# Value rows of 40 instead of 32 tokens gathered and summed on VectorE in a mixture-of-experts decoder layer

## The chip, the cores and the metric

One Trainium2 chip, one of its cores. The metric is the device time of one execution in microseconds (us), from launch to end; runs of the same kernel vary by some 0.3%. TensorE (PE in the profile) multiplies, VectorE (DVE), ScalarE (ACT) and GpSimd (POOL) do elementwise work, and SyncE (SP) only issues transfers here. GpSimd issues the indirect transfers (gathers and scatters by an index).

## The reference

One decoder layer over 256 tokens of width 1024, in fp32: a mixer (a gated linear recurrence beside attention), a cross-attention into 256 memory tokens, and a PEER channel mixer; then a last RMSNorm. The change lies in the PEER part alone:

```python
q = (t @ w_q).reshape(T, 8, 2, 128)                     # 8 heads, two halves
s = einsum('thpd,hpnd->thpn', q, sub_keys)              # 128 keys a half
s_top, i_top = top_k(s, 16)                             # then the 256 sums of pairs
best_s, pos = top_k(cand_s, 16)                         # 16 experts a head: 128 a token
ids   = ...                                             # i * 128 + j, of 16384 experts
gates = softmax(best_s)
act = gelu(einsum('td,ted->te', x_c, u[ids_c]))
y   = einsum('te,ted->td', gates * act, v[ids_c])
```

Each token uses 128 of 16384 experts. An expert has a row of `u` and a row of `v`, 1024 numbers each.

## The kernel before, in words

**Dense instead of sparse.** The kernel computes all 16384 activations of every token. It goes over j = 0..127; "key" j stands for the 128 experts i * 128 + j, one to a partition. In the *u stage* TensorE computes for each key the scores of 128 experts against 256 tokens (8 chunks of the width, 3 products each, lines 1431 to 1433), ScalarE takes the GELU of them. In the *v stage* it multiplies, for each key, the 128 rows of `v` with the weighted activations and sums over all keys in eight PSUM banks. Weights are exact to fp32 by splitting each operand in a high and a low fp32r part: ScalarE writes the high part (line 702), VectorE the low part (lines 1021 and 1028), so each key needs a load (SP), a split on ScalarE and one on VectorE before TensorE can use it. Four slots rotate: a row is loaded again into a slot as soon as its split is done (SP waits for `s_vl`), and ScalarE splits into a slot when TensorE has finished the key four before (`s_vm`).

**Three kinds of tokens.** What multiplies the activations is a token's gate where it uses the expert, and zero elsewhere.
- `WT` = 192 tokens get it from a map in DRAM, `wmap`, into which GpSimd scatters the gates (line 431, 192 indirect transfers), and which comes back two keys at a time (`wblk`, 64 loads); VectorE multiplies (L1155, function `weigh`; GpSimd does the first four, L437).
- `OT` = 32 tokens (one-hot tokens) get it inside the u stage: from key 95 (`ROUTE0`) on, every second key, a group of `GRP` = 4 tokens. VectorE and ScalarE build two one-hot matrices a token, TensorE multiplies them (L1454, 4 products a group), VectorE places the result (`place`); activations that come after it are multiplied by `late_gelu`.
- `NS` = 32 tokens (sparse tokens) don't take part in the dense product of the v stage. Their activations are stored to DRAM (`adump`, five pieces). When all is there, GpSimd gathers with 32 indirect transfers the activations that each sparse token needs (L447: 128 numbers a transfer, one to a partition), and then with 32 more the rows of `v` (L452: 128 rows of 4 KB, three buffers `vg`). VectorE multiplies each gathered tile by a weight for each partition and adds it up in `acc_s` (L1166, `sparse_fma`). A token has P / NS = 4 partitions, and each of these holds 32 of its 128 experts. Near the end TensorE sums the 4 partitions of each token by a product with a 0/1 matrix `sel` (L1507).

**Columns.** So the v stage has `DT` = 256 - 32 = 224 tokens. For each key and chunk there are two products: high part of `v` with both parts of the activations, 448 columns (L1479), and low part with the high part, 224 columns (L1480). The last two keys are done chunk by chunk, three products of 224 columns each (L1490), so that the end of the kernel can start early.

**Order around the change.** All queues are written by hand. VectorE's loop over keys holds the splits, the remaining routing (top-k) and the gates; the last batch of gates (tokens 128 to 255) comes at key 78. At that point it also copies the sparse tokens' expert numbers and gates to their four partitions (`sparse_rows`: eight copies of 32 partitions). In the v stage VectorE does for each key the low part of `v`, for each second key `weigh` and the low part of the weighted activations (L1150), and the sparse products are laid in by

```python
FMA0, NVG = 34, 3
def fma_step(c):
    return FMA0 + c * (KEYS - 4 - FMA0) // NSD      # 32 steps, keys 34 to 121
```

GpSimd's order in the v stage: four multiplications, 32 activation gathers, then the 32 row gathers, each of which waits until the product three before is done (`s_fma`). SP's order at the end of u: the first four `v` rows, a wait for the scatters, four weight blocks, the last dump.

Of the kernel before, what the change touches and what calls it, by code (L numbers as in the profile page):

```python
# [13 lines left out]
F32 = mybir.dt.float32  # L14
# [8 lines left out]
P = 128  # L23
# [56 lines left out]
def build(nc, x, mem, par, wa, wx, w, keys_t, u_t, v, wmap, adump, xres, out):  # L80
    ctx = ExitStack()
    with ctx:
        base = 16512

        def at(name, off, shape, dt=F32):
            return nc.alloc_sbuf_tensor_at(name, [P] + shape, dt, offset=base + off)

        def sem(name):
            return ctx.enter_context(nc.semaphore(name))
# [4 lines left out]
        act_w = at("act_w", 16 * K, [KEYS, DT])  # L94
# [30 lines left out]
        gate_s = at("gate_s", m + 384, [NSD])  # L125
        idx_v = at("idx_v", m + 512, [NSD], U32)
        idx_a = at("idx_a", m + 640, [NSD], U32)
        late = at("late", m + 768, [2, OT])
        aw_s = at("aw_s", m + 1024, [NSD])
        w_s = at("w_s", m + 1152, [NSD])  # L130
        sel = at("sel", m + 4352, [NS])
        wblk = at("wblk", m + 1280, [2, WBK, WT])
# [37 lines left out]
        def flat(ap):  # L170
# [41 lines left out]
        s_ad, s_ag, s_ws, s_fma, s_al = (sem(n) for n in (  # L212
            "s_act_dumped", "s_act_gathered", "s_sparse_weights", "s_sparse_fma", "s_al_sums"))
# [76 lines left out]
        def vbank(c):  # L290

            return acc[:, c] if c < 4 else bank[c - 4]
# [9 lines left out]
        def _(sp):  # L302
# [77 lines left out]
        def _(pool):  # L380
# [65 lines left out]
            for c in range(NSD):  # L446
                nc.gpsimd.indirect_dma_start(out=aw_s[:, c:c + 1], out_offset=None, in_=adump,  # L447
                                             in_offset=bass.IndirectOffsetOnAxis(ap=idx_a[:, c:c + 1], axis=0)).then_inc(s_ag, 16)
            for c in range(NSD):
                if c >= NVG:  # L450
                    pool.wait_ge(s_fma, c - NVG + 1)
                nc.gpsimd.indirect_dma_start(out=vg[:, c % NVG], out_offset=None, in_=v,  # L452
                                             in_offset=bass.IndirectOffsetOnAxis(ap=idx_v[:, c:c + 1], axis=0)).then_inc(s_vg[c % NVG], 16)
# [334 lines left out]
        def _(dve):  # L788
# [70 lines left out]

            dve.wait_ge(s_spc, 1)  # L860
# [201 lines left out]
            def sparse_rows(dst, src):  # L1062
                nr = NSD // PH
                to, fr = (a.rearrange("p (h k) -> p h k", h=PH) for a in (dst[:], src[:]))
                for r in range(TOPK // nr):
                    last = V.tensor_copy(to[NS * r:NS * r + NS], fr[P - NS:P, :, nr * r:nr * r + nr])
                link(last)

            def gates(b):
# [4 lines left out]
                if t == 1:  # L1074
                    sparse_rows(idx_v, dest)
# [50 lines left out]
            for r in range(P // NS):  # L1126
                q = slice(NS * r, NS * r + NS)
                last = V.tensor_scalar(tcol[q, 2:3], tcol[q, 0:1], float(-NS * r), None, ALU.add)
            link(last)
            V.tensor_scalar(sel[:], iota[:, 0:NS], tcol[:, 2:3], None, ALU.is_equal)  # L1130
# [26 lines left out]
            def sparse_fma(c):  # L1157
                if c == 0:
                    dve.wait_ge(s_ag, 16 * NSD)
                    V.tensor_tensor(w_s[:], gate_s[:], aw_s[:], ALU.mult).then_inc(s_ws, 1)  # L1160
                    dve.wait_ge(s_ws, 1)
                dve.wait_ge(s_vg[c % NVG], 16 * (c // NVG + 1))
                w = w_s[:, c:c + 1]
                if c:
                    dve.wait_ge(s_fma, c)
                    V.scalar_tensor_tensor(acc_s[:], vg[:, c % NVG], w, acc_s[:], ALU.mult, ALU.add).then_inc(s_fma, 1)  # L1166
                else:
                    V.tensor_scalar(acc_s[:], vg[:, 0], w, None, ALU.mult).then_inc(s_fma, 1)

            parts, batches = PARTS0, EARLY  # L1170
            for j in range(KEYS):
# [16 lines left out]
                if j == ROUTE0 - 2:  # L1188
                    dve.wait_ge(s_kte, 1)
                if j + 2 in range(ROUTE0, ROUTE0 + 2 * NGRP, 2):  # L1190
                    onehots_i((j + 2 - ROUTE0) // 2)
# [28 lines left out]
        def _(pe):  # L1220
# [283 lines left out]
            def sparse_sums():  # L1504
                pe.wait_ge(s_fma, NSD)
                for c in range(DC):
                    pe.matmul(vbank(c)[:, DT:T], acc_s[:, P * c:P * c + P], sel[:], start=False, stop=False,  # L1507
                                     skip_group_check=True)
# [65 lines left out]
```

## Time and profile before

| | |
|---|---|
| median of 3 runs | 1010.39 us (1008.94 to 1011.98) |
| the profiled execution | 1010.26 us, span 1008.5 us |
| granted TensorE clock, mean | 0.995 |
| PE busy | 986.9 us (98%) |
| DVE busy | 749.5 us (74%) |
| ACT busy | 549.6 us (55%) |
| POOL busy | 430.7 us (43%) |
| transfers | 225.58 MB, mean 224 GB/s |

The span runs from the first to the last instruction of the profiled execution; its own time is 1.8 us longer. "Busy" of PE is time in which a product is in flight, and products overlap; how much TensorE does is read from the distances between starts. The u stage lies at about 292 to 669 us, the v stage at 669 to 998.

### The profile page before, as it was taken

Reading aid. Unit: us, or ns where it says so; the run is one execution under the profiler, and the core shown is the slowest. Engines: PE = TensorE matmul, PEld = TensorE weight load, DVE = VectorE, ACT = ScalarE, POOL = GpSimd, SP = SyncE. Lnnn points to the kernel's source line nnn. Section 1 sums busy time; section 2 is a strip of 40 time slices with the busy share of each in tenths; the row PEclk is TensorE's granted clock in tenths of the full one; section 3 lists DMA queues with packets and bytes.
Section 4 is the critical chain, followed back from the end, with each engine's and each line's share of the span. In section 5 each row is a group of like instructions: output and inputs, shape, how many; then the busy total and the mean of one; then the engine's idle time right before and its main releaser. Section 6 shows DMA issues by size and latency. Waiting matters only on the chain.

```text
span 1008.5 us, 19138 instructions
## 1 busy us (share of the span) xinstructions
PE 986.9 (98%) x7455; PEld 958.8 (95%) x7455; DVE 749.5 (74%) x1466; ACT 549.6 (55%) x986; POOL 430.7 (43%) x286
## 2 busy tenths in 40 slices
PE   7999999999999999999999999999999999999996
PEld 7998999999999999999999999999999999999996
DVE  5756665544999999998985566457668888888883
ACT  6785555545455545444454675545555555555543
POOL 1000001001288888888878888857401121121200
PEclk9999999999999999999999999999999999999998
DMA  9689664524547777877777777877878999999971
GB/s 311 203 305 323 223 220 160 190 84 148 187 84 171 178 197 193 202 189 186 201 175 198 175 183 160 202 244 263 297 261 288 318 318 329 313 334 331 316 246 43
DMA packets 129546, 225.58 MB, mean 224 GB/s; under 512 B 36560, under 2 KB 84816, under 8 KB 129360
## 3 DMA queue, kind: packets, MB, share of 16 engines
q1 hardware_dynamic: 96208, 207.95, 62.4%
q0 software_dynamic: 33280, 16.91, 11.7%
q8 instruction: 30, 0.49, 0.2%
q14 instruction: 28, 0.23, 0.1%
HBM read 207.94 MB, written 16.88 MB: 223 GB/s over the span
## 4 chain that ended last, share of the span: by engine, by line
PE 88%; DVE 8%; ACT 2%; issue 1%; DMA 1%; SPq 0%; DVEq 0%; ACTq 0%
PE acc L1260 20%; PE acc L1479 11%; PE bank L1479 11%; PE bank L1431 10%; PE bank L1432 10%; PE bank L1433 10%; PE acc L1480 5%; PE bank L1480 5%; DVE hl L1028 2%; PE bank L1454 1%; DMA wraw<-w_in 1%; DVE wsp L800 1%; PE bank L1371 1%; PE bank L1415 1%; PE bank L1349 1%
## 5 line engine op out<-in xcount | busy, mean ns | idle before, releaser
L431 POOL DMA_INDIRECT wmap<-gate,widx x192 | 325.1, 1693 | 97.4 <-issue 60.0
L702 ACT ACTIVATE hl<-raw 128x1024 fp32r<-128x1024 f32 x192 | 203.7, 1061 | 90.4 <-PE bank L1480 83.3
L1431 PE MATMUL bank<-xt,hl 128*128 128x256 f32 x768 | 218.2, 284 | 1.3 <-DVE hl L1021 0.8
L1432 PE MATMUL bank<-xt,hl 128*128 128x256 f32 x768 | 217.2, 283 | 0.0
L1433 PE MATMUL bank<-xt,hl 128*128 128x256 f32 x768 | 217.1, 283 | 0.0
L1021 DVE TENSOR_TENSOR hl<-raw,hl 128x1024 fp32r<-128x1024 f32 x99 | 121.2, 1225 | 59.3 <-ACT hl L702 57.9
L1028 DVE TENSOR_TENSOR hl<-raw,hl 128x512 fp32r<-128x512 f32 x186 | 119.4, 687 | 44.7 <-ACT hl L702 43.4
L1431 PEld LDWEIGHTS bank<-xt,hl 128*128 128x128 f32 x768 | 147.1, 191 | 1.7 <-DVE hl L1021 1.0
L1432 PEld LDWEIGHTS bank<-xt,hl 128*128 128x128 f32 x768 | 147.2, 192 | 0.0
L1433 PEld LDWEIGHTS bank<-xt,hl 128*128 128x128 f32 x768 | 147.2, 192 | 0.0
L707 ACT ACTIVATE act_w<-bank 128x224 f32<-128x224 f32 (+6 forms) x128 | 45.1, 353 | 165.8 <-PE bank L1433 165.7
L452 POOL DMA_INDIRECT vg<-v,idx_v x32 | 45.9, 1434 | 198.1 <-DVE acc_s L1166 153.8
L1479 PE MATMUL acc<-whl,hl 128*128 128x448 f32 x380 | 124.9, 373 | 0.8 <-DVE whl L1150 0.8
L1479 PE MATMUL bank<-whl,hl 128*128 128x448 f32 x380 | 124.7, 372 | 0.0
L800 DVE TENSOR_TENSOR wsp<-wraw,wsp 128x2048 fp32r<-128x2048 f32 x35 | 80.2, 2290 | 58.0 <-ACT wsp L462 57.8
L1260 PE MATMUL acc<-xt,wsp 128*128 128x256 f32 x960 | 118.9, 285 | 2.9 <-DVE xt L824 2.9
L1260 PEld LDWEIGHTS acc<-xt,wsp 128*128 128x128 f32 x960 | 116.5, 191 | 3.6 <-issue 3.5
L462 ACT ACTIVATE wsp<-wraw 128x2048 fp32r<-128x2048 f32 x35 | 66.9, 1912 | 79.7 <-PE acc L1260 79.7
L1480 PE MATMUL acc<-whl,hl 128*128 128x224 f32 x380 | 100.3, 264 | 0.0
L1480 PE MATMUL bank<-whl,hl 128*128 128x224 f32 x380 | 100.3, 264 | 0.0
L1479 PEld LDWEIGHTS acc<-whl,hl 128*128 128x128 f32 x380 | 71.4, 188 | 6.2 <-DVE hl L1021 0.9
L1479 PEld LDWEIGHTS bank<-whl,hl 128*128 128x128 f32 x380 | 71.3, 188 | 5.3
(263 smaller groups left out, 1953.5 us busy)
## 6 DMA issues: line engine op xcount, KB each, us to landing
raw<-u_t SPq DMA_DIRECT2D x128, 512.0 KB, 4.4
raw<-v SPq DMA_DIRECT2D x128, 512.0 KB, 5.1
wmap<-zeros SPq DMA_DIRECT2D x6, 2048.0 KB, 11.7
wblk<-wmap SPq DMA_DIRECT2D x64, 192.0 KB, 5.3
wraw<-w_in SPq DMA_DIRECT2D x9, 1024.0 KB, 8.7
wraw<-w_pq SPq DMA_DIRECT2D x8, 1024.0 KB, 5.3
wraw<-w_ck SPq DMA_DIRECT2D x4, 1024.0 KB, 8.0
wraw<-w_cv SPq DMA_DIRECT2D x4, 1024.0 KB, 7.9
```

The lines of the kernel that those rows point to most:

```text
L431: nc.gpsimd.indirect_dma_start(out=wmap, out_offset=bass.IndirectOffsetOnAxis(ap=set_ranks(widx, k)[:, h, r:r + 1], axis=0), in_=set_ranks ...
L462: nc.scalar.activation(wsp[:, u % 2, 0], wraw[:, u % WRAW], ACT.Copy).then_inc(s_wh, 1)
L702: nc.scalar.activation(eslot(k, 0, second), raw[:, k // 2, k % 2], ACT.Copy).then_inc(ready, 1)
L800: V.tensor_tensor(wsp[:, u % 2, 1], wraw[:, u % WRAW], wsp[:, u % 2, 0].bitcast(F32), ALU.subtract).then_inc(s_wl, 1)
L1021: V.tensor_tensor(eslot(k, 1, second), raw[:, k // 2, k % 2], eslot(k, 0, second).bitcast(F32), ALU.subtract).then_inc(ready, 1)
L1028: last = V.tensor_tensor(eslot(k, 1, False)[:, q], raw[:, k // 2, k % 2, q], eslot(k, 0, False)[:, q].bitcast(F32), ALU.subtract)
L1260: last = pe.matmul(dst, a, b, start=(c == c0 and n == 0), stop=(c == c1 - 1 and n == 2))
L1431: pe.matmul(dst, uh[:, c], xt[:, c, 0], start=(c == 0), stop=False)
L1432: pe.matmul(dst, uh[:, c], xt[:, c, 1], start=False, stop=False)
L1433: last = pe.matmul(dst, ul[:, c], xt[:, c, 0], start=False, stop=(c == DC - 1))
L1479: pe.matmul(both, vh[:, q], whole, start=first, stop=False, skip_group_check=True)
L1480: last = pe.matmul(both[:, 0], vl[:, q], whole[:, 0], start=False, stop=False, skip_group_check=True)
```

## The change

40 tokens are sparse instead of 32, 24 are one-hot tokens instead of 32, the map keeps its 192. So the v stage has 216 tokens. A sparse token has 3 partitions instead of 4 (`NR` = 128 // 40), 120 partitions are used, and each holds 43 of its 128 experts (`NSD` = 43; one place of 129 is padding with weight zero and expert zero). As three times 40 partitions don't lie on the 32-partition borders, the numbers and gates are brought to their places through DRAM: VectorE puts them into `stage_i` and `stage_g`, SP stores them (ahead of key 89's load) and loads them in the new order (ahead of key 97's). VectorE computes the gather addresses at key 107. The activation gathers are cut into groups of 8 with semaphores of their own: the first 8 stand before the row gathers, the rest go in fours between them. The sparse products begin at key 12, 43 of them in 112 keys.

```diff
-NS = 32
+NS = 40
-HT = P - 2 * NS
-OT = 32
+HT = 64
+OT = P - HT - NS
-NSD = NS * PH * TOPK // P
-FMA0, NVG = 34, 3
+NR = P // NS
+NSP = NR * NS
+NSD = -(-PH * TOPK // NR)
+ACTB = 8
+FMA0, NVG = 12, 3
...
+                if j == 88:
+                    sp.wait_ge(s_stg, 1)
+                    for far, near in ((sgate, stage_g), (sidx, stage_i)):
+                        sp.dma_start(far.rearrange("(r t c) o -> t r (c o)", r=NR, t=NS),
+                                     near[P - NS:P, :].rearrange("t (r c) -> t r c", r=NR)).then_inc(s_sst, 16)
+                if j == 96:
+                    sp.wait_ge(s_sst, 32)
+                    for far, near in ((sgate, gate_s), (sidx, idx_v)):
+                        sp.dma_start(near[0:NSP, :], far.rearrange("(p c) o -> p (c o)", p=NSP)).then_inc(s_sbk, 16)
...
+            pool.wait_ge(s_ix, 1)
+            def act_rows(c0, c1):
+                for c in range(c0, min(c1, NSD)):
+                    nc.gpsimd.indirect_dma_start(out=aw_s[0:NSP, c:c + 1], out_offset=None, in_=adump,
+                                                 in_offset=bass.IndirectOffsetOnAxis(ap=idx_a[0:NSP, c:c + 1], axis=0)).then_inc(s_ag[c // ACTB], 16)
+            act_rows(0, ACTB)
             for c in range(NSD):
                 if c >= NVG:
                     pool.wait_ge(s_fma, c - NVG + 1)
-                nc.gpsimd.indirect_dma_start(out=vg[:, c % NVG], out_offset=None, in_=v,
+                nc.gpsimd.indirect_dma_start(out=vg[0:NSP, c % NVG], out_offset=None, in_=v,
...
+                if c >= NVG - 1:
+                    act_rows(ACTB + 4 * (c - NVG + 1), ACTB + 4 * (c - NVG + 2))
...
+            dve.wait_ge(s_const, 11)
+            token, part = tcol[:, 2:3], tcol[:, 0:1]
+            link(V.tensor_scalar(token, part, float(NS), float(-NS), ALU.is_ge, ALU.mult))
+            link(V.tensor_tensor(token, token, part, ALU.add))
+            for r in range(2, NR):
+                over = tcol[:, 4:5]
+                link(V.tensor_scalar(over, part, float(NS * r), float(-NS), ALU.is_ge, ALU.mult))
+                link(V.tensor_tensor(token, token, over, ALU.add))
+            V.tensor_scalar(sel[:], iota[:, 0:NS], token, None, ALU.is_equal)
...
                 if t == 1:
-                    sparse_rows(idx_v, dest)
+                    V.memset(stage_g[:, PH * TOPK:], 0.0)
+                    V.memset(stage_i[:, PH * TOPK:].bitcast(F32), 0.0)
+                    link(V.tensor_copy(stage_i[:, 0:PH * TOPK], dest[:]))
...
                 if t == 1:
-                    sparse_rows(gate_s, krow[:, t, 2])
-                    link(V.tensor_scalar(idx_a[:], idx_v[:], float(NS), tcol[:, 2:3], ALU.mult, ALU.add))
+                    V.tensor_copy(stage_g[:, 0:PH * TOPK], krow[:, t, 2]).then_inc(s_stg, 1)
...
-                if c == 0:
-                    dve.wait_ge(s_ag, 16 * NSD)
-                    V.tensor_tensor(w_s[:], gate_s[:], aw_s[:], ALU.mult).then_inc(s_ws, 1)
-                    dve.wait_ge(s_ws, 1)
+                if c % ACTB == 0:
+                    b, cs = c // ACTB, slice(c, min(c + ACTB, NSD))
+                    dve.wait_ge(s_ag[b], 16 * (cs.stop - cs.start))
+                    V.tensor_tensor(w_s[q, cs], gate_s[q, cs], aw_s[q, cs], ALU.mult).then_inc(s_ws, 1)
+                    dve.wait_ge(s_ws, b + 1)
...
+                if j == ROUTE0 + 2 * NGRP:
+                    q = slice(0, NSP)
+                    dve.wait_ge(s_sbk, 32)
+                    V.tensor_scalar(idx_a[q], idx_v[q], float(NS), tcol[q, 2:3], ALU.mult, ALU.add).then_inc(s_ix, 1)
```

## Rows read from the trace of the kernel before

**Rows 1.** Busy time by stretch: us, busy of each engine, granted clock, transfer share, GB/s.

```profile
400.00:500.00 100.00, 100.00 (x840) 100.00 (x839) 93.09 (x258) 48.80 (x105) 85.37 (x49) 1.00 0.78 196
700.00:750.00 50.00, 50.00 (x321) 47.77 (x320) 34.55 (x41) 25.87 (x30) 16.45 (x18) 1.00 0.84 280
...
760.00:960.00 200.00, 200.00 (x1279) 191.05 (x1278) 169.59 (x189) 103.59 (x120) 42.02 (x28) 1.00 0.92 320
```

**Rows 2.** The waits of TensorE: us in total, times, longest.

```profile
PE bank L1431 <- DVE hl L1021: 0.8, 1, 0.8
PE acc L1479 <- DVE whl L1150: 0.8, 1, 0.8
```

**Rows 3.** TensorE's products in order of time: start, us; first two of a key, next key.

```profile
800.89 0.37 PE L1479 MATMUL acc<-whl,hl3v 128*128 128x448 f32 x1
801.10 0.26 PE L1480 MATMUL acc<-whl,hl3v 128*128 128x224 f32 x1
...
803.39 0.37 PE L1479 MATMUL acc<-whl,hl 128*128 128x448 f32 x1
```

**Rows 4.** The chain that ended last, near the end: start, us, what.

```profile
987.36 0.89 PE bank L1507 x8
...
990.83 2.01 PE acc L1490 x18
```

**Rows 5.** TensorE's weight loads in order of time, same key as rows 3.

```profile
801.10 0.19 PEld L1479 LDWEIGHTS acc<-whl,hl3v 128*128 128x128 f32 x1
801.21 0.19 PEld L1480 LDWEIGHTS acc<-whl,hl3v 128*128 128x128 f32 x1
```

**Rows 6.** The chain that ended last: first of eight groups, and the hand-over to v.

```profile
569.85 0.89 PE bank L1454 x8
...
668.72 0.55 DVE whl L1150
```

**Rows 7.** GpSimd in order of time: start, us, operation, idle before it.

```profile
665.03 2.50 POOL L437 TENSOR_TENSOR act_w<-act_w,wblk 128x384 f32<-128x384 f32 x2 [8.07 <-DMA wblk<-wmap]
...
694.05 0.95 POOL L447 DMA_INDIRECT aw_s<-adump,idx_a  x1 [0.31 <-issue]
...
932.77 1.86 POOL L452 DMA_INDIRECT vg<-v,idx_v  x1 [5.97 <-DVE acc_s L1166]
```

**Rows 8.** VectorE in order of time: after the softplus chain, and in batch 4's gates.

```profile
48.80 2.29 DVE L800 TENSOR_TENSOR wsp<-wraw,wsp 128x2048 fp32r<-128x2048 f32 x1 [3.90 <-ACT wsp L462]
...
523.85 0.75 DVE L1066 CAST idx_v<-dest 32x32 uint32<-32x32 f32 x4
...
525.84 0.85 DVE L1066 COPY gate_s<-krow 32x32 f32<-32x32 f32 x4
```

**Rows 9.** VectorE's groups, 760 to 960 us: busy us, mean ns, idle before.

```profile
L1021 DVE TENSOR_TENSOR hl<-raw,hl 128x1024 fp32r<-128x1024 f32 x60 | 73.5, 1224 | 26.0 <-ACT hl L702 24.8
L1166 DVE SCALAR_TENSOR_TENSOR acc_s<-vg,w_s,acc_s 128x1024 f32<-128x1024 f32 x28 | 35.8, 1278 | 0.0
L1150 DVE TENSOR_TENSOR whl<-act_w,whl 128x448 fp32r<-128x448 f32 x40 | 24.7, 618 | 0.0
...
L1155 DVE TENSOR_TENSOR act_w<-act_w,wblk 128x384 f32<-128x384 f32 x39 | 21.5, 550 | 1.6 <-DMA wblk<-wmap 1.6
```

**Rows 10.** GpSimd's gathers by group: busy us, mean ns, idle before (row gathers: 760 to 960).

```profile
L452 POOL DMA_INDIRECT vg<-v,idx_v x28 | 42.0, 1501 | 191.0 <-DVE acc_s L1166 147.6 <-DVE acc_s L1168 43.4
...
L447 POOL DMA_INDIRECT aw_s<-adump,idx_a x32 | 36.5, 1140 | 9.6 <-issue 9.5
```

**Rows 11.** Transfers: GB/s in 40 slices of 690 to 740; landing times, 760 to 960.

```profile
GB/s 256 312 257 343 315 159 36 102 312 112 326 256 295 138 291 242 301 145 281 270 302 154 325 243 331 390 324 308 371 404 421 411 357 326 266 264 306 154 288 233
...
raw<-v SPq DMA_DIRECT2D x80, 512.0 KB, 5.3
...
vg<-v,idx_v POOLq DMA_INDIRECT x28, 7.3
```

**Rows 12.** The page's costliest groups: ScalarE's split of a row of u or v.

```profile
L702 ACT ACTIVATE hl<-raw 128x1024 fp32r<-128x1024 f32 x192 | 203.7, 1061 | 90.4 <-PE bank L1480 83.3
```

More of the change, by code:

```diff
@@ L77, with build @@
 ROUTE0 = 95
-def build(nc, x, mem, par, wa, wx, w, keys_t, u_t, v, wmap, adump, xres, out):
+def build(nc, x, mem, par, wa, wx, w, keys_t, u_t, v, wmap, adump, sgate, sidx, xres, out):
     ctx = ExitStack()
@@ L124, in build @@
         kt3 = at("kt3", m, [3, OT])
[L125 to L132, printed above, removed]
+        gate_s = at("gate_s", m + 288, [NSD])
+        idx_v = at("idx_v", m + 480, [NSD], U32)
+        idx_a = at("idx_a", m + 672, [NSD], U32)
+        late = at("late", m + 864, [2, OT])
+        aw_s = at("aw_s", m + 1056, [NSD])
+        w_s = at("w_s", 16 * K, [NSD])
+        stage_g = at("stage_g", m + 1344, [NR * NSD])
+        stage_i = at("stage_i", m + 1344 + 544, [NR * NSD], U32)
+        wblk = at("wblk", m + 1344, [2, WBK, WT])
+        sel = at("sel", m + 4416, [NS])
         cand = at("cand", m, [256])
@@ L211, in build @@
         s_uh, s_ul, s_um, s_ua = (sem(n) for n in ("s_u_high", "s_u_low", "s_u_mm", "s_u_gelu"))
-        s_ad, s_ag, s_ws, s_fma, s_al = (sem(n) for n in (
-            "s_act_dumped", "s_act_gathered", "s_sparse_weights", "s_sparse_fma", "s_al_sums"))
+        s_ad, s_ws, s_fma, s_al = (sem(n) for n in ("s_act_dumped", "s_sparse_weights", "s_sparse_fma", "s_al_sums"))
+        s_stg, s_sst, s_sbk, s_ix = (sem(n) for n in (
+            "s_sparse_staged", "s_sparse_stored", "s_sparse_back", "s_sparse_index"))
+        s_ag = [sem(f"s_act_gathered{i}") for i in range(-(-NSD // ACTB))]
         s_vg = [sem(f"s_v_rows{i}") for i in range(NVG)]
@@ L445, in _ @@
             pool.wait_ge(s_ad, 16 * 5)
-            for c in range(NSD):
-                nc.gpsimd.indirect_dma_start(out=aw_s[:, c:c + 1], out_offset=None, in_=adump,
-                                             in_offset=bass.IndirectOffsetOnAxis(ap=idx_a[:, c:c + 1], axis=0)).then_inc(s_ag, 16)
+            pool.wait_ge(s_ix, 1)
[4 more added lines that the diff above has]
+            act_rows(0, ACTB)
             for c in range(NSD):
@@ L1060, in route_part @@
                     V.tensor_scalar(krow[:, t, 2, ks], topv[:, 2], topv[:, 2, 0:1], None, ALU.subtract).then_inc(s_rt, 1)
[L1062 to L1067, printed above, removed]
             def gates(b):
@@ L1124, in route_parts @@
                     route_part(p // 4, p % 4)
[L1126 to L1130, printed above, removed]
             for u in range(U_PQ, NU - 2):
@@ L1506, in sparse_sums @@
                 for c in range(DC):
-                    pe.matmul(vbank(c)[:, DT:T], acc_s[:, P * c:P * c + P], sel[:], start=False, stop=False,
+                    pe.matmul(vbank(c)[:, DT:T], acc_s[0:NSP, P * c:P * c + P], sel[0:NSP], start=False, stop=False,
                                      skip_group_check=True)
@@ L1570 @@
     w = {k: ap[k] for k in ("w_in", "w_ck", "w_cv", "w_out", "w_cq", "w_co", "w_pq")}
-    build(nc, ap["x"], ap["mem"], ap["par"], ap["wa"], ap["wx"], w, ap["keys_t"], ap["u_t"], ap["v"], wmap, adump, xres, out)
+    build(nc, ap["x"], ap["mem"], ap["par"], ap["wa"], ap["wx"], w, ap["keys_t"], ap["u_t"], ap["v"], wmap, adump, sgate, sidx, xres, out)
     r = run(nc, [arrays], core_ids=[0])
```

13 lines of the change are left out of this document (8 added, 5 removed).

## The prediction

> **What bounds the kernel now.** I read the busy time by stretch first [rows 1]. In the first product of the expert stage (the u stage, 292 to 669 us) and in the second one (the v stage, 669 to 998 us) TensorE is busy for the whole of every stretch at a granted clock of 1.00, its upper level of 2.4 GHz, while VectorE is idle for 15% of the v stage (169.59 of 200 us busy). The waits of TensorE [rows 2] say the same: over 700 us of expert work it waits for others in a few places, each under 1 us, once in the first splits of u (0.8 us) and once at the hand-over from u to v (0.8 us). So time is won only where TensorE gets less to do, and lost only where another engine or a transfer becomes later than its lead. In the v stage each of 128 keys costs eight pairs of products: L1479 streams 448 columns (both halves of the weighted activations, 2 x 224 tokens), L1480 224. Key after key starts 2.50 us later (800.89 to 803.39) [rows 3], 0.313 us a pair.
>
> **What the change takes from TensorE.** The dense part shrinks from 224 to 216 tokens: L1479 has 432 columns, L1480 216. 126 of the keys run as pairs, which makes 1008 pairs.
>
> Two readings of the price of a column are possible. By proportion: a pair of 672 columns takes 0.313 us, 0.466 ns a column, and the u stage gives the same (840 products of 256 columns in 100 us, 0.119 us each, 0.465 ns a column [rows 1]). Then 24 columns are 11.2 ns a pair and 11.3 us in all. By a floor: a product that streams little doesn't step faster than its weights are loaded. The eight records with 32 columns take 0.89 us, 0.111 each, and the 18 products of 224 columns near the end take 2.01 us, 0.112 each, where proportion would give 0.104 [rows 4]. In a pair, the weight load of L1479 starts together with the product L1480 (801.10 in [rows 3, 5]), and the next load starts 0.11 us later [rows 5]: L1480 lasts just as long as that load. With 216 columns it streams 3 to 4 ns less and still has the load to wait for. Then only the 16 columns of L1479 count: 16 x 0.466 = 7.5 ns at most, 16 / 2.4 = 6.7 ns at least, so 6.7 to 7.5 us over 1008 pairs. I take the floor, because [rows 4] have a stream of exactly this width that is slower than proportion allows, and 7.1 us of it. Both ends, 6.7 and 11.3, go into the range.
>
> The Trainium skill (TensorE: Matmul & The Clock Gate, LDWEIGHTS (loading the stationary operand)) says that a weight load costs its number of columns over 1.2 GHz, which is 107 ns for 128; by that rule the trace's 0.111 to 0.112 is the load and little beside it, and L1480 gives nothing back. The same page (Back-to-back issue gap) prices an isolated product at its columns over 2.4 GHz plus 2.5 ns; by that alone the pair would save 10 ns and the stage 10.1 us, and the trace's 0.112 for 224 columns speaks against it.
>
> The last two keys (L1490, 48 products of 224 columns, now 216) stand at the floor already: nothing. The sparse sums (L1507) go from 32 to 40 columns at 0.111 a record: nothing.
>
> The one-hot tokens fall from 32 to 24, eight groups to six. Each group is a piece of 0.89 us (L1454) that lies bare on the chain [rows 6]; two go: 1.8 us. With them go two placements and some late multiplications on VectorE, off the path.
>
> Does this 1.8 us survive the hand-over from u to v? Before, TensorE starts v when VectorE has split the first weights (0.55 us at 668.72) [rows 6]. Those need GpSimd's multiplication at 665.03, which waited 8.07 us for the weight block [rows 7]; the block in turn waits for the last scatters, which GpSimd issues back to back and which don't come earlier. v starts at 669.3 (668.72 + 0.55) after 0.8 us of idle, so u ends at 668.5, and at 666.7 after the change. The first multiplication is done at 665.03 + 1.25 = 666.3, half of the two in that row; then some 0.6 us on ScalarE and 0.55 on VectorE give 667.5, which is 1.8 us before 669.3. So the saving is just kept, with nothing to spare: should the block come later by 1 us, 1 us of it is lost.
>
> **What the change adds, and its cover.** *Making the order through DRAM.* Batch 4's gates lose eight copies of 32 partitions (0.75 and 0.85 us [rows 8]) and an index operation, and get two small memsets and two copies of 128 columns: about even, on VectorE, which has slack there. SP gets two stores before key 89's load and two loads before key 97's, some 0.3 us of issue each. The stores wait for gates that VectorE writes at key 78, ten keys before; the loads wait for the stores, eight keys (24 us) later; VectorE picks up at key 107, eleven keys later. Behind SP's waits stand the u rows, behind VectorE's wait the splits; all three are met long before, so 0. Had a wait not been met, TensorE would starve after its lead of about three keys. The token numbers move to VectorE's first stage (some six operations of 0.15 to 0.24 us, 1 us), ahead of the chain after which VectorE waits 3.90 us for ScalarE [rows 8]: 0.
>
> *VectorE in v.* By the rows [rows 9] a key cost 1.224 for the split, half of (0.618 + 0.550) for a pair of weight columns, and 1.278 every 90/32 = 2.81 keys: 2.26 us. Records overlap, and the busy time of [rows 1] is 169.6/200 x 2.505 = 2.12, 0.94 of it. Now 43 row products stand in 112 keys, one in 2.605: 1.224 + 0.575 + 0.491 = 2.29, times 0.94 = 2.15 us in a key of 2.505 - 0.056 = 2.45: 88% where it was 85%. It remains covered. It begins at key 12 instead of 34, where VectorE was 31% idle (700 to 750 in [rows 1]).
>
> *GpSimd's queue.* The first eight activation gathers start where they did, near 672; then come three row gathers and four more activations: 15 in a row at up to 1.5 + 0.3 us, ready near 699. VectorE comes to the first row product when TensorE ends key 12: 13 keys of 2.45 us and the residual's products after the start at 667.5, 703 or later. From then each step of 2.605 x 2.45 = 6.4 us asks GpSimd for one row gather and four activation gathers, for eight steps. At the shortest, 0.95 us plus 0.31 of issue [rows 7], a step costs 6.3; at the mean of the 32 activation gathers (1.140) 7.2; at the mean of the row gathers beside a full VectorE (1.501) 9.0 [rows 10]. A row gather is issued three steps (19.1 us) ahead and lands after 7.3 [rows 11]: 11.8 us of slack. Eight steps at 7.2 are 6.4 us late in all, hidden; at 9.0 they are 21 late, 9 over the slack; TensorE's lead of three keys less the 2.3 us for splitting (1.061 us on ScalarE [rows 12], 1.224 on VectorE; 5 us remain) and what VectorE catches up (0.3 us a key over ten keys, 3 us) leave 1 us. I take 0, and 1 to 2 for the range.
>
> *Transfers.* A key now moves 512 + 96 + 480/2.605 = 792 KB, 811 thousand bytes, in 2.45 us: 331 GB/s against 320 [rows 1]. In stretches of 1.25 us side by side the queues did 371, 404, 421, 411 and 357 [rows 11], so there is room; the rows of v land after 5.3 us where a slot is refilled right after its split, some 3 us into the four keys until ScalarE needs it: 6.8 us. Cost 0, with a rival below.
>
> **Sum.** 7.1 + 1.8 = 8.9 us off the profiled execution, whose own time is 1010.26 (span 1008.5, 1.8 around it): 1001.4. The median of the three runs shown is 0.13 above that execution: 1001.5.
>
> **Rivals.**
> 1. Columns in proportion. All 24 pay: 11.3 + 1.8 = 13.1, 997.3. For it: u and v agree on 0.466 ns. Against it: 0.112 for 224 columns. 0.20.
> 2. Forecast: the floor holds, the rest is hidden, 1001.5 (own range 1000.4 to 1002.6). 0.54.
> 3. Gathers partly late: the queue at 9 to 9.5 us a step, some 1 to 5 us of TensorE idle near keys 30 to 45: 1002.5 to 1006.5. 0.09.
> 4. The transfers are the bound. At 92% busy [rows 1] they may not go past what they do. At 322 GB/s 811 thousand bytes take 2.52 us, 0.014 more than a key takes now; over 110 keys that is 1.6 us, which eats the routes' saving: 1010. Against it are the slices above 400. 0.08.
> 5. Slower: VectorE stands in order behind a row gather that GpSimd's queue issues late. Many row gathers took 1.86 us [rows 7]; with 0.30 of issue a step then asks 10.8 us: 8 x 4.4 = 35 us late, less 11.8, 5 and 3, is 15 us of idle TensorE: 1016. It decides from about 2.0 us a gather on: 8 x (10 - 6.4) - 19.8 = 9. Against it: a late VectorE is idle, and beside a half idle VectorE the gathers took 0.95 [rows 7]. 0.06, and 0.03 for a loss of this size that I don't see.
>
> **How the numbers follow.** A measurement of this kernel can't tell less than 0.3% (3 us) from no change: faster is below 1007.4, slower above 1013.4. Faster: cases 1, 2, 3: 0.83. Same: case 4 and an edge of 3 and 5: 0.09. Slower: 0.08. The range runs from just under case 1 to the end of case 3: 996.5 to 1007.0, leaving out 0.17.
>
> **What will show it.** Pairs: starts of L1479 and L1480 0.205 then 0.105 to 0.11 apart if the floor holds, 0.302 for a pair if proportion does; keys 2.44 or 2.42 us apart. Six pieces of L1454. VectorE near 88% busy from key 12 on, without a wait for gathered rows. If TensorE waits for VectorE around 745 to 775 us, case 3 or 5 is right; if ScalarE waits for rows of v throughout, case 4.

## The result: 1.7% slower, and where the time went

The changed kernel takes 1027.87 us (median of four runs, 1020.67 to 1034.93) against 1010.30 of the kernel before: ratio 1.0167, 95% interval 1.0134 to 1.0200. The forecast was 1001.5 with a range to 1007.0, so the sign was wrong too. Ratios here and below compare undisturbed executions alone, so they can differ a little from the quotient of the medians. The four executions fall into two pairs, 1020.67 and 1022.37, 1033.37 and 1034.93. The profiled one is of the first pair: 1022.37 us (span 1020.6), 12.1 more than that of before. What the second pair lost beyond that is seen in the profile of `after_again` below.

Busy time by stretch, changed kernel, columns as in [rows 1]:

```profile
400.00:500.00 100.00, 100.00 (x840) 100.00 (x839) 93.26 (x255) 48.56 (x106) 85.69 (x48) 1.00 0.78 195
700.00:750.00 50.00, 50.00 (x327) 48.63 (x326) 42.75 (x50) 26.97 (x33) 33.77 (x24) 1.00 0.98 308
750.00:800.00 50.00, 45.65 (x283) 43.55 (x282) 36.59 (x42) 21.23 (x25) 29.31 (x22) 0.97 0.94 274
760.00:960.00 200.00, 190.11 (x1190) 179.40 (x1189) 161.22 (x181) 97.66 (x111) 52.50 (x39) 0.99 1.01 303
800.00:950.00 150.00, 144.46 (x909) 135.84 (x908) 123.61 (x141) 75.99 (x86) 28.69 (x22) 1.00 1.02 309
```

In 400 to 500 TensorE starts the same 840 products as before. The loss is in v: in 760 to 960 TensorE gets 1190 products started where it got 1279 [rows 1]. TensorE in order of time, first product and last pair of v, in the kernel before and then in the changed one:

```profile
669.40 0.44 PE L1479 MATMUL acc<-whl,hl 128*128 128x448 f32 x1 [0.76 <-DVE whl L1150]
...
990.57 0.26 PE L1480 MATMUL bank<-whl,hl 128*128 128x224 f32 x1
```

```profile
666.96 0.44 PE L1507 MATMUL acc<-whl,hl 128*128 128x432 f32 x1 [1.49 <-DVE whl L1172]
...
1002.49 0.37 PE L1507 MATMUL bank<-whl,hl 128*128 128x432 f32 x1
```

v begins 2.4 us earlier (of these, 1.5 lie ahead of the u stage, whose first product came at 290.06 instead of 291.54; the version with 128 rows below began it at 291.83 in one profile and at 293.33 in another, so these 1.5 are not the change's). From its first product to the second of its last pair (0.21 after the line of 1002.49) it lasts 335.7 us where it lasted 321.2: 14.5 lost less 2.4 won is the 12.1. The waits in 650 to 1021 say for whom (us in all, times, longest):

```profile
ACT hl L725 <- DMA raw<-v: 62.1, 48, 5.2
...
ACT hl3v L725 <- DMA raw<-v: 23.7, 23, 2.7
DVE act_w L1177 <- DMA wblk<-wmap: 18.6, 19, 3.4
...
DVE acc_s L1190 <- DMA vg<-v,idx_v: 7.2, 4, 2.4
PE acc L1507 <- DVE hl L1054: 7.2, 12, 3.0
```

ScalarE waits 71 times for rows of v; in the kernel before, the same waits were 5.8 and 3.5 us in five times. TensorE waits for the split behind it. The chain that ended last confirms it: between 780 and 850 us it steps from transfer to transfer.

```profile
780.59 1.24 DVE hl L1054
781.84 10.48 DMA raw<-v
792.35 1.07 ACT hl L725
793.44 1.24 DVE hl L1054
794.69 8.81 DMA raw<-v
```

So the slot of `raw` is refilled as soon as VectorE leaves it (781.84), and the rows take 8.8 to 10.5 us to arrive. The queues (the 16 that move all transfers; their busy share is the last but one number of a window) are full (share 1.02 in 800 to 950, where before had 0.93) and yet deliver less: 309 GB/s, against 322 of the kernel before in the same stretch. The page's landing times, against [rows 11]:

```profile
raw<-v SPq DMA_DIRECT2D x128, 512.0 KB, 6.9
wblk<-wmap SPq DMA_DIRECT2D x64, 192.0 KB, 7.4
```

Before, the page had 5.1 and 5.3. A full queue that moves less means a dearer byte, not more bytes. That is the puzzle for the experiments.

### The profile page after: what moved, and what is told of

The parts are those of the page before. It is cut to its first block, busy times and chain, and to the rows that moved or that the text cites. A ratio compares the mean times of both kernels' runs of the same rounds, so it can differ in the third digit from the quotient of the medians.

```text
span 1020.6 us, 19130 instructions
## 1 busy us (share of the span) xinstructions
PE 988.3 (97%) x7439; PEld 959.0 (94%) x7439; DVE 756.0 (74%) x1466; ACT 547.1 (54%) x976; POOL 467.7 (46%) x308
## 4 chain that ended last, share of the span: by engine, by line
POOL 37%; PE 24%; DMA 15%; DVE 10%; issue 10%; ACT 4%; SPq 0%; DVEq 0%; ACTq 0%; POOLq 0%
POOL wmap L447 32%; PE acc L1288 17%; DMA raw<-v 9%; DMA wblk<-wmap 4%; POOL aw_s L466 4%; DVE hl L1054 2%; ACT hl L725 2%; DVE acc_s L1190 1%; DVE wsp L823 1%; POOL vg L473 1%; PE acc L1507 1%; PE bank L1507 1%; DMA vg<-v,idx_v 1%; DVE act_w L1177 1%; DVE whl L1172 1%
## 5 line engine op out<-in xcount | busy, mean ns | idle before, releaser
L473 POOL DMA_INDIRECT vg<-v,idx_v x43 | 58.1, 1351 | 179.9 <-DVE acc_s L1190 160.4
L1507 PE MATMUL acc<-whl,hl 128*128 128x432 f32 x380 | 125.8, 378 | 9.0 <-DVE hl L1054 7.2
L730 ACT ACTIVATE act_w<-bank 128x216 f32<-128x216 f32 (+4 forms) x128 | 44.3, 346 | 165.3 <-PE bank L1461 165.1
L1507 PE MATMUL bank<-whl,hl 128*128 128x432 f32 x380 | 124.0, 373 | 0.0
L1508 PE MATMUL acc<-whl,hl 128*128 128x216 f32 x380 | 100.0, 263 | 0.0
L1508 PE MATMUL bank<-whl,hl 128*128 128x216 f32 x380 | 100.0, 263 | 0.0
L766 ACT ACTIVATE whl<-act_w 128x432 fp32r<-128x432 f32 x64 | 36.2, 566 | 77.6 <-DVE act_w L1177 75.1
```

The costliest lines, as they stand in the source:

```text
L473: nc.gpsimd.indirect_dma_start(out=vg[0:NSP, c % NVG], out_offset=None, in_=v, in_offset=bass.IndirectOffsetOnAxis(ap=idx_v[0:NSP, c:c + 1 ...
L1507: pe.matmul(both, vh[:, q], whole, start=first, stop=False, skip_group_check=True)
L1508: last = pe.matmul(both[:, 0], vl[:, q], whole[:, 0], start=False, stop=False, skip_group_check=True)
```

## The experiments

Each of four groups ran on one chip beside the kernel before; ratios are to that. A group's times are best compared with each other. The theories: **A**, a row gather over 120 of the 128 partitions costs the queues more than one over 128; **B**, the demand (a gather in 2.6 keys, shorter keys) is too much; **C**, GpSimd's queue issues the gathers late.

**Gathers over 128 partitions.** Eight idle partitions fetch row 0 of v; sum and products stay at 120.

```diff
-  indirect_dma_start(out=vg[0:NSP, c % NVG], ..., ap=idx_v[0:NSP, c:c + 1] ...)
+  indirect_dma_start(out=vg[:, c % NVG], ..., ap=idx_v[:, c:c + 1] ...)
+  link(V.memset(idx_v[:].bitcast(F32), 0.0))      # in the gates of batch 4
```

> The changed kernel, but each row gather fetches 128 rows instead of 120: partitions 120 to 127 take row 0 of v, and nothing uses them. Theory A (a gather over 120 partitions costs the transfer queues more than one over 128: 1.88 us of the 16 queues against 1.60): the row transfers fall back to about 1.6 us each though they move 7% more, rows of v land in 5.5 us again, and the time is 1001 to 1005. Theory B (the demand is too high: a product every 2.6 keys and shorter keys bring the queues to their limit): still more bytes, so 1022 or more. Theory C (GpSimd's queue of interleaved gathers makes VectorE late): no change, about 1020 to 1028.

Measured: 1004.19 us (1002.37 to 1007.86), ratio 0.9942 (0.9923 to 0.9962). 7% more bytes a gather, 24 us less than the changed kernel's median (30 us less on one chip with it, last group). Its windows and its first and last pair of v:

```profile
750.00:800.00 50.00, 50.00 (x326) 48.59 (x325) 44.12 (x50) 26.09 (x30) 25.86 (x19) 1.00 0.96 347
800.00:950.00 150.00, 150.00 (x975) 145.78 (x975) 132.14 (x149) 78.78 (x91) 31.79 (x23) 1.00 0.95 334
```

```profile
668.63 0.43 PE L1508 MATMUL acc<-whl,hl 128*128 128x432 f32 x1 [1.48 <-DVE whl L1173]
...
984.54 0.26 PE L1509 MATMUL bank<-whl,hl 128*128 128x216 f32 x1
```

TensorE is full again, 334 GB/s go through at a share of 0.95, and a row of v lands after 5.6 us. B falls: the demand is higher here. C as the main cause falls: GpSimd issues the same list.

**The kernel before with gathers over 120 and over 112 partitions.** `vg[0:120]`, `idx_v[0:120, ...]`, and so in the products and the sum; the last tokens' parts are left out. Likewise 112.

> The kernel before, but each row gather fetches only 120 rows and the products and the sum use 120 partitions; the part of the sum that the last 8 partitions hold is left out. Nothing else changes, and 6% fewer bytes are gathered. Theory A: the gathers cost the queues 1.85 us instead of 1.6, landing times rise from 7.3 to 9 us, and the time goes up, to 1012 to 1022 (a full key has 0.05 us more of its own than in the changed kernel, so less than there). Theory B and C: 1010 or a little less, landing times at 7.3 us or under.

> The kernel before with row gathers, products and sum over 112 partitions, a multiple of 16; what the last 16 partitions hold is left out. Theory A in its form that the rows must divide evenly over 16 queues: as before, 1010, a gather at 1.4 us of the queues. Theory A in its form that anything under 128 partitions breaks the match of queue and partition: slower, 1012 to 1022. Theories B and C: 1010 or less.

Measured: 120: 1014.59 us, ratio 1.0034 (1.0015 to 1.0052). 112: 1009.42 us, 0.9991 (0.9976 to 1.0006). One edit, 32 KB less a gather, takes the kernel before from 322 to 292 GB/s in 800 to 950 (in its profiled execution, 1020.48 us, the slowest of ten from 1011.00 on). VectorE waits for no gather in it, ScalarE 64.3 us for rows of v:

```profile
800.00:950.00 150.00, 144.98 (x910) 136.22 (x910) 118.86 (x132) 74.37 (x84) 25.14 (x20) 1.00 1.02 292
```

So A holds without any other part of the change. I read from the pair that a row count that is a multiple of 16 is cheap. That reading fell later.

**The changed kernel without row gathers and row products** (`acc_s` set to zero: the 40 tokens' sums are left out).

> The changed kernel without the row gathers and the products of VectorE (the 40 sparse tokens get no expert sum; the activation gathers stay). All theories: the transfers have room, TensorE is the bound, and the time shows what the columns and the two groups give by themselves: with the floor of the weight load 1001 to 1002, with all 24 columns paying 997 to 998. If it is above 1003, something outside the row gathers costs time.

Measured: 1003.88 us, 0.9933 (0.9915 to 0.9951), the time of the version with 128. Gathers over 128 partitions are hidden altogether. I had expected 1001 to 1002; the 2 to 3 us above that are the columns and the hand-over to v, which gave less than forecast (last part of the next section).

**On a second chip: 90 partitions, all gathers at 128, a shorter product, a later start.** There the kernel before took 1026.65 us (1010.23 to 1033.09), so these four are compared above all with each other. `before_rows90` is the kernel before with `0:90`, `all128` fetches the activations over 128 partitions too, `low128` cuts L1509 to 128 of its 216 columns (the weights' low part is left out for 88 tokens), `rows128_from34` sets `FMA0, NVG = 34, 3` back.

```diff
-  last = pe.matmul(both[:, 0], vl[:, q], whole[:, 0], ...)
+  last = pe.matmul(both[:, 0, 0:P], vl[:, q], whole[:, 0, 0:P], ...)     # low128
```

> The kernel before with row gathers, products and sum over 90 partitions; what the other 38 hold is left out, and 30% fewer rows are gathered. It tells how a gather's rows are dealt out to the 16 transfer queues. Theory A1 (over the largest number of queues up to 16 that divides the rows: 15, six rows each): no queue carries more than in the kernel before, 1008 to 1010. Theory A2 (over the largest power of two that divides them: 2 queues with 45 rows each; for 120 rows it would be 8 queues with 15): each gather puts 184 KB on two queues that have 38 KB a key to carry besides, about 100 KB a key at some 23 KB a us is 4.5 us a key over 90 keys, so 1100 or far above. Theory A3 (only the remainder over 16 counts, one row more on some queues): 1008 to 1012.

> The changed kernel with 128 rows in each row gather and 128 numbers in each activation gather too. The activation gathers carry 4 bytes a row; under theory A their spread over the queues costs little: the same as with 128 rows alone, 1003 to 1005. If their count of 120 mattered as well, 1001 to 1003.

> The changed kernel with 128-row gathers, and the product of the low part of v (216 columns) cut to 128 columns; the low part is left out for the other tokens. Theory floor (that product lasts as long as the next weight load, 0.107 to 0.11 us, whatever it streams): the pair stays at 0.307 us and the time at 1002 to 1004.5. Theory proportion (0.466 ns a column, or 0.417 at the clock): 88 columns are 37 to 41 ns a pair, 37 to 41 us over 1008 pairs; ScalarE, VectorE and the transfers then become the bound, at 2.3 us a key or so, which would leave about 985 to 990.

> The changed kernel with 128-row gathers, with the 43 products laid in from key 34 as before (one in 2.09 keys) instead of from key 12 (one in 2.6). Bytes a key: 512 + 96 + 512/2.09 = 853 KB, 873 thousand in 2.47 us, 354 GB/s; VectorE 1.224 + 0.575 + 0.611 = 2.41, times 0.94 is 2.27 of 2.47. If the early start matters, the queues or VectorE are the bound there and the time is 1006 to 1015; if there is room for that too, 1003 to 1005.

Measured: 1028.21, 1009.24, 1007.20 and 1015.67 us. With 90 the kernel before is at 1.0058 (0.9986 to 1.0130) of itself: a dealing by powers of two, which would have put it near 1100, is out, though it is far above the 1008 to 1010 I had written down, as the kernel before is on this chip. `all128`, expected at 1003 to 1005, shows no gain from wider activation gathers. Its profiled execution lacks 39 products in 750 to 800, where VectorE waited 6.3 us for one row gather: even at 128 a gather can come late there, as it did in neither profile of the version with 128. `low128` answers the question of the price of columns: its window holds 981 products in 150 us, that of `all128` 976:

```profile
800.00:950.00 150.00, 150.00 (x981) 146.24 (x979) 132.56 (x150) 79.47 (x93) 33.43 (x24) 1.00 0.95 337
```

A key (16 products) takes 2.447 instead of 2.459 us; 88 columns less in each of eight short products give 0.012 us, 1.5 ns a product. In proportion they would have given 41 ns. (Its total says less: in 700 to 775 its profiled execution lost products for another reason, TensorE standing without a wait that the profile shows.) `rows128_from34`, 0.7 us above my range, is 6.4 us slower than `all128`: with the same 43 gathers squeezed behind key 34, TensorE waits twice for a split, 8.1 us.

**The changed kernel with 112, 105, 104 and 96 partitions.** `0:NSP` becomes `0:112` and so on in gather, products and sum; the last rows' parts are left out.

> The changed kernel with its row gathers, products and final sum over the first 112 of the 120 partitions (it leaves out the last 8 partial rows, so the sums of the tokens from 37 on are short). Theory 'the dealing': a gather whose row count is no multiple of 16 is what makes transfers dear; 112 is one (16 queues, 7 rows each), so this runs as the version with 128 rows does, about 1004 us, 1.5% or more under the kernel before when measured together, 960 pieces or more of TensorE work in 800 to 950, a fetch of rows of v near 5.5 us. Rival 'the amount': fewer bytes are what helps or hurts; then it lies at the changed kernel's 1020 to 1028 us or a little under, with the keys' fetches at 6.5 us or more.

> The same with 105 partitions. Theory 'the dealing' by the largest divisor up to 16: 15 queues with 7 rows each, as 120 is 15 queues with 8 each, so it is dear again: 1012 to 1025 us in the scale of the first chip, at least 8 us more than with 112, though it fetches 7 rows fewer; the row gathers' queue time is above that of 112. If only the number of rows counted: at or under the time of 112.

> The same with 104 partitions. Largest divisor: 13 queues with 8 rows each, three queues with none, the starts rotating: the dearest for its size, at least as slow as 105, and 24 short filling packets a gather (128 data-carrying or filling packets, 144 with the 16 that signal). Rival form of the dealing, rounding up to 7 rows a queue (14 queues with 7, one with 6, one with none): 8 filling packets a gather, 128 in all, and a time between that of 105 and of 112. If only the number of rows counted: under 112.

> The same with 96 partitions: 16 queues with 6 rows each. Dealing: fast, like 112 or up to 2 us less, about 1003 us in the scale of the first chip; the 4 us that were left on transfers elsewhere do not come back. Amount: in line with 104 and 105, a little under them.

Measured: 112: 1023.42 us, 1.0111 (1.0077 to 1.0145). 105: 1022.38, 1.0135 (1.0075 to 1.0195). 104: 1036.54, 1.0236 (1.0173 to 1.0298). 96: 1011.11, 1.0013 (0.9985 to 1.0042). "A multiple of 16 is enough" fails at 112, and hardly holds at 96, which should have been 1003. That the count of queues alone orders the times fails too: 105 should have been at least 8 us slower than 112 and was 1 us faster. It does count between neighbours: 104 has one row less than 105 and is 14 us slower. The packets show the dealing. Packets of the whole execution with 128, 120 and 104 partitions:

```profile
DMA packets 132013, 231.96 MB, mean 231 GB/s; under 512 B 37618, under 2 KB 85874, under 8 KB 131826
```

```profile
DMA packets 132013, 230.56 MB, mean 226 GB/s; under 512 B 37962, under 2 KB 86218, under 8 KB 131826
```

```profile
DMA packets 132013, 227.74 MB, mean 219 GB/s; under 512 B 38650, under 2 KB 86906, under 8 KB 131826
```

The short packets grow by 344 = 43 x 8 and by 1032 = 43 x 24 over the version with 128: 8 fillers a gather with 120 (15 queues of 8 rows, one with fillers alone), 24 with 104 (13 queues of 8, three with fillers). So the number of queues is the largest divisor of the row count up to 16. (With 90 the short packets grow by 192 = 32 x 6, with two halves by 512 = 32 x 16: the 16 packets of a gather that signal.)

The Trainium skill (DMA: Bandwidth & Descriptors, Why a DMA increments its semaphore by 16 and not by 1) states this: the slowest dimension is cut into the largest number of shares, 16 at most, that divides it. By that rule the trace's 8 and 24 fillers are one and three queues without a row; it agrees.

**Both versions again on one chip, and two gathers of 64 for one of 128.** The last is the kernel before; both halves fetch the rows of the first 64 partitions, so the bytes stay and the second half's sums use other rows.

```diff
-  indirect_dma_start(out=vg[:, c % NVG], ..., ap=idx_v[:, c:c + 1] ...)
+  for h in (0, 64):
+      indirect_dma_start(out=vg[h:h + 64, c % NVG], ..., ap=idx_v[0:64, c:c + 1] ...)
```

> The changed kernel as it is, on the same chip as the next two. With 120 rows a gather: 1020 to 1028 us, the row gathers at 1.9 to 2.1 us of the queues each in 800 to 950.

> The version with all 128 rows fetched, again. If only a gather of all 128 partitions is cheap: 1002 to 1008 us here too, at least 10 us under each of the other two, 1.55 to 1.6 us a gather and the other transfers' packet time near 1.9% a megabyte. If the 1.5% that rows112 lacked was that chip's: rows112_again lies within 4 us of this one.

> The changed kernel with 112 partitions gathered, again (it leaves out the last 8 partial rows). 'Only 128 rows are cheap' (each queue then writes its own eighth of the partitions): 1012 to 1025 us. 'A multiple of 16 is enough, the last chip was at fault': 1002 to 1008 us.

> The kernel before with each row gather of 128 partitions made by two gathers of 64, both with the row numbers of the first 64 partitions (so the second half's rows are other rows; the bytes are the same). 64 is a multiple of 16, 4 rows a queue. 'Only 128 rows are cheap': the two cost together more than the 1.59 us of queue time of the one, 1.8 us or more, and the other transfers' packet time rises from 1.9 to 2.0% a megabyte or more; 1010 to 1022 us. 'A multiple of 16 is enough': 1.59 to 1.7 us (16 more signalling packets), 1.9% a megabyte, 1009 to 1011 us.

Measured: 1033.25 us, 1.0228 (1.0209 to 1.0246); 1003.63, 0.9932 (0.9913 to 0.9951); 1023.56, 1.0097 (1.0063 to 1.0131); 1027.01, 1.0181 (1.0138 to 1.0224). `after_again` and `before_halves` are 5 us above my ranges, the other two as expected for "only 128 rows are cheap". The profiled execution of `after_again` took 1036.36 us, as long as those of the second pair in the result. VectorE waits only 0.4 us for gathers there, ScalarE 101 us for rows of v, and TensorE starts 882 products in 800 to 950:

```profile
800.00:950.00 150.00, 141.07 (x882) 133.02 (x881) 120.94 (x137) 73.94 (x84) 31.28 (x22) 0.99 1.02 298
```

So in that execution the loss is the queues' without VectorE's waits for gathers. The chip was not at fault for 112. And with the halves neither the bytes nor a multiple of 16 can be all that counts: VectorE waits for no gather there, and it is the same 512 KB a step, 16 queues for each half, 17 us slower. They have 16 short signalling packets more a step, and a filler or signal is short beside a row of 4 KB; that these alone cost it is not excluded by this run, but 112 rows have no more of them than 128 and are dear too. Queues in 800 to 950 of the kernel before, with halves, of the changed kernel and of that with 128 (packets, MB, share of the 16 queues' time; q0 carries the gathers alone there, q1 all else):

```profile
q1 hardware_dynamic: 12935, 37.28, 70.6%
q0 software_dynamic: 3024, 11.01, 22.3%
```

```profile
q1 hardware_dynamic: 11546, 33.31, 75.4%
q0 software_dynamic: 3180, 10.46, 28.0%
```

```profile
q1 hardware_dynamic: 12385, 35.65, 73.5%
q0 software_dynamic: 3140, 10.70, 28.9%
```

```profile
q1 hardware_dynamic: 13017, 37.59, 70.6%
q0 software_dynamic: 3431, 12.49, 24.7%
```

With n packets a gather (rows, fillers, 16 that signal) the packets give the number of gathers, and the share times 150 us, divided by that number, the queue time of one (all 16 busy). For 128 rows: 3024 / 144 = 21 gathers, 33.5 / 21 = 1.59 us. Kernels so read:

```
kernel           rows x queues   us a gather   ns a row   q1, % per MB   GB/s
before             128 x 16         1.59          12.4        1.89        322
rows128            128 x 16         1.55          12.1        1.88        334
rows128_again      128 x 16         1.60          12.5        1.85        336
before_rows112     112 x 16         1.50          13.4        1.99        314
rows96              96 x 16         1.39          14.5        2.00        318
rows112            112 x 16         1.70          15.2        2.08        310
before_halves       64 x 16         1.06          16.6        2.26        292
before_rows90       90 x 15         1.27          14.1        2.05        300
rows105            105 x 15         1.62          15.4        2.01        325
after              120 x 15         1.99          16.6        2.06        309
after_again        120 x 15         2.08          17.3        2.13        298
before_rows120     120 x 15         2.08          17.3        2.18        292
rows104            104 x 13         1.75          16.8        2.16        294
```

Only gathers over all 128 partitions cost 12.1 to 12.5 ns a row (`all128` and `low128`, read in the same way, give 12.4 and 12.3); every other shape costs 13.4 to 17.3, and makes the direct transfers beside it 5 to 20% dearer a byte. That is not only the crowding of full queues: `before_rows112` and `before_rows90` have TensorE full and a share of 0.95 and 0.94, as with 128 rows, and pay 1.99 and 2.05% a megabyte where that pays 1.88.

The table is not the whole of the times, though. Against the version with 128, these products are missing in 750 to 800 and in 800 to 950: in the changed kernel 43 and 66, with 112 partitions 100 and 43, with 105 83 and 4, with 104 126 and 68, with 96 49 and none. With 96 to 112 most of the loss, with 105 and 96 nearly all of it, lies before 800, where the queues had room (shares 0.73 to 0.87). With 112:

```profile
750.00:800.00 50.00, 38.96 (x226) 37.17 (x225) 27.71 (x32) 16.10 (x20) 38.93 (x25) 0.86 0.74 227
DVE acc_s L1190 <- DMA vg<-v,idx_v: 21.1, 3, 7.5
```

VectorE (second line, 740 to 800) stands for row gathers that land 7.5 us after their issue, where they take 7.4 with 128; they are issued late. GpSimd needs 1.8 to 2.3 us for one there, not 1.4 (last section). So for these four theory C, in the form that GpSimd takes longer over such a gather, explains more than the queues do, and their totals can't be used to rank shapes by queue time. In the kernel before, 112 did no harm although GpSimd needed 1.87 us a gather too: there no activation gathers stand between the row gathers, and the queues kept some room (0.95).

## Why the prediction was wrong

**The step that failed** is *Transfers*: "Cost 0". It priced a gather by its bytes, 480 KB where it was 512, so less. The number that counts is queue time: 1.99 us where it was 1.59, and 2.06% a megabyte on everything else where it was 1.89. In 150 us the 16 queues can give about 1.02 of their time (1.04 was the most, with the halves); a key of the changed kernel asks 2.46 / 150 of it, or 1.64%. It moves 512 + 96 KB directly (0.623 MB, 1.28%) and 1.99 / 2.605 = 0.76 us of gathers (0.51%): 1.79%, 9% more than there is at a share of 1.00, 7% at 1.02. TensorE's products in that stretch fell by 7% (909 for 975). With the prices of 128 rows the same key asks 1.17 + 0.40 = 1.57%, and fits. The prices are read from the same stretches, so this is a balance and not an independent test; the tests are the versions with 128 and 120 rows. I used slices above 400 GB/s as proof of room; they were stretches without the dear gathers' company.

Rival 4 (the transfers are the bound, 0.08) had the place and the sign to look for, "ScalarE waits for rows of v throughout", and that is what the trace shows. Its price, 1010, was made of the same bytes and was 18 us short.

The Trainium skill (DMA: Bandwidth & Descriptors, Why a DMA increments its semaphore by 16 and not by 1; The descriptor swizzle) gives the dealing, and says of a transfer of 1 MiB to 128 partitions that each queue writes eight partitions (not an eighth, as one expectation has it), those of one port of its own. I did not weigh it when I predicted, though by it 120 rows go to 15 queues. That the match of queue and port is what makes 128 cheap fits the table, halves included, but no view here shows which queue writes which partition, so it is argued and not shown. How 15 queues or halves of 64 make the other transfers dearer stays open.

**GpSimd's queue**, "hidden, 0", was wrong too. In 709 to 768 us the seven steps took 8.4 us each (709.20 to 768.17), where 7.2 was my middle and 9.0 my high value; with gathers over 128 they took 7.7 (708.54 to 762.59). More than half of the 4.9 us between the two is one gather that held GpSimd for 4.14 us (725.46); why is not known. And a row gather landed 9.1 us after its issue, not 7.3 [rows 11]. VectorE in order of time, changed kernel:

```profile
759.21 0.16 DVE L1184 TENSOR_TENSOR w_s<-gate_s,aw_s 120x8 f32<-120x8 f32 x1
762.45 1.30 DVE L1190 SCALAR_TENSOR_TENSOR acc_s<-vg,w_s,acc_s 120x1024 f32<-120x1024 f32 x1 [3.08 <-issue]
```

```profile
753.26 0.97 POOL L473 DMA_INDIRECT vg<-v,idx_v  x1 [0.30 <-issue]
```

```profile
765.41 0.47 PE L1507 MATMUL acc<-whl,hl 128*128 128x432 f32 x1 [3.04 <-DVE hl L1054]
```

The gather issued at 753.26 is needed at 759.4 and lands near 762.4 (the row names no releaser; that it is this gather is read from the order and the 9.1 us). VectorE stands 3.1 us, the split behind it is late, and TensorE stands 3.0 us. So the issue had fallen to one step ahead of the use, and case 3 happened, in the place named (745 to 775). Against the version with 128, 43 products are missing in 750 to 800 (6.6 us at 0.154 a product) and 66 in 800 to 950 (10.2 us); together 16.8 of the 18.1 between the two profiled executions. In the first part gathers and blocks both come late; how much each takes is not separated. Case 5's mechanism, VectorE behind a late gather, is strongest with 112 partitions, where VectorE waited 26.7 us in four times; there GpSimd issued slowly (below).

**Columns: the floor** holds. In the version with 128, v lasts 984.54 - 668.63 = 315.9 us where it lasted 321.2: 5.3 us, 5.2 ns a pair. The forecast was 7.1 (6.7 to 7.5), so the term was oversized by 1.8. Rival 1 (11.3, 0.20) is out, and `low128` shows why: columns of the short product are all but free. In both kernels the second product starts 0.21 after the first; 16 columns gave 5.2 ns where 6.7 was my least, which I can't explain from these rows.

**Routes**: six pieces of 0.89 where eight were. From its first product to its last the u stage takes 375.1 us in the changed kernel and with 128 rows, where it took 376.8: 1.7 to 1.8, as forecast. **Hand-over**, "nothing to spare": right in kind. TensorE stands 1.49 us before v instead of 0.76 in the changed kernel, and 1.48 with 128 rows, so 0.7 of the 1.8 is lost; in `after_again` it stood 0.73 and lost none.

**VectorE at 88%**: 132.14 of 150 us with 128 partitions, 88%. **The order made through DRAM, gates, tcol**: no wait of TensorE on them in any version; 0 held.

With the gathers at 128 the sum is 1.8 - 0.7 + 5.3 = 6.4 us, and 1004.30 against 1010.26 is 6.0; its u stage began 0.3 us later. The forecast would have been 2.7 us off for that kernel (median 1004.19); the rest of the miss, 23.7 us, goes with the gathers' shape.

## What to carry to other kernels

Price a transfer by the time that it takes of the queues, not by its bytes: when full queues move fewer GB/s than before, a byte has become dearer. Before making an indirect gather over fewer than 128 partitions in a stretch whose queues are nine tenths full, fill it up to 128 with rows that nobody reads; here the 7% more bytes took 24 us off. Look also at how long GpSimd needs to issue such a gather, and whether it is issued late: that costs where the queues are not full. The version with 128 (1004.19 and 1003.63 us, ratios 0.9942 and 0.9932) is faster than both kernels of this case.

## What the runs showed of the hardware that I had not expected

- The gather's shape, as in the table: 1.59 us of queue time for 128 rows, 2.08 for 120, and 2 x 1.06 for twice 64, with the direct transfers 9 to 20% dearer beside the last two.
- GpSimd takes longer to issue a gather over 90 to 112 partitions. In 700 to 950 us, changed kernel with 112 partitions, then with 128:

```profile
L473 POOL DMA_INDIRECT vg<-v,idx_v x34 | 71.9, 2114 | 114.4 <-DVE acc_s L1190 96.7 <-DVE acc_s L1192 14.6 <-issue 3.1
```

```profile
L473 POOL DMA_INDIRECT vg<-v,idx_v x38 | 52.5, 1381 | 150.5 <-DVE acc_s L1191 134.9 <-DVE acc_s L1193 12.9 <-issue 2.8
```

  With 105 and 104 the mean was 2264 and 2294 ns, with 96 1817, but with 120 1355. The kernel before has the same: 1434 with 128, 1245 with 120, 1872 with 112, 1877 with 90. I have no explanation for that order.
- A stall of TensorE cost some clock behind it as well. After the idle 3.0 us at 762.4 to 765.4 the changed kernel's TensorE started six pairs of products 0.57 us apart instead of 0.31, at a granted clock of 0.51, its lower level of 1.2 GHz; that is 1.5 us more. From 770 to 775 the clock was 1.00 again.

```profile
766.16:769.55 3.39, 3.39 (x14) 3.21 (x13) 3.39 (x5) 2.06 (x3) 2.78 (x3) 0.51 0.73 282
```
